# A wait that paces VectorE by GpSimd, and a sparser order of convolution taps, layer norm and top-k, in a two-layer hybrid decoder step on one core

## The reference

```python
def mixer_layer(x, c, q_pos, top_k, ...):
    shift, scale, gate = jnp.split(jax.nn.silu(c) @ w_ada + b_ada, 3, axis=-1)
    h = rms_norm(x, norm_g) * (1 + scale[:, None]) + shift[:, None]
    zq, zk, zv, zqi, zki, zwi, zga, zglu, zgc, zmerge = split_in(h @ w_in)
    ...
    attn = ...            # indexer scores, top-k keys per query, softmax over them
    y_att = (attn * jax.nn.silu(zga)) @ w_attn_out
    za, zb = jnp.split(zglu, 2, axis=-1)
    u = za * jax.nn.sigmoid(zb)
    d = lax.conv_general_dilated(conv_in, conv_w, ...) + conv_b     # causal, depthwise, 31 taps, 1024 channels
    d = layer_norm(d, conv_ln_g, conv_ln_b)
    y_conv = (jax.nn.silu(d) * jax.nn.silu(zgc)) @ w_conv_out
    g_att, g_conv = jnp.split(jax.nn.sigmoid(zmerge), 2, axis=-1)
    return x + gate[:, None] * ((g_att * y_att + g_conv * y_conv) @ w_out), ...
```

## Time and profile before

| | us |
|---|---|
| median of 3 runs | 3767.42 |
| lowest, highest | 3760.27, 3771.24 |
| the profiled execution | 3748.51 |
| its span | 3746.7 |
| PE busy | 3517.2 (94%) |
| DVE busy | 1797.4 (48%) |
| POOL busy | 1217.4 (32%) |
| ACT busy | 1065.2 (28%) |

### The profile page before, as it was taken

How to read it: one execution, slowest core, us unless ns; L and a number is a source line. 1 busy time by engine, 2 the same in 40 slices (tenths; PEclk the granted TensorE clock), 3 DMA queues, 4 the chain that set the end, 5 groups by cost and what they waited for, 6 DMA issues and landing times. The chain is left out here.

```text
span 3746.7 us, 66701 instructions
## 1 busy us (share of the span) xinstructions
PE 3517.2 (94%) x27774; PEld 3257.7 (87%) x27774; DVE 1797.4 (48%) x2508; ACT 1065.2 (28%) x1494; POOL 1217.4 (32%) x476
## 2 busy tenths in 40 slices
PE   5699999989899899999998999998988999999999
PEld 2499988878889889898887999897888898889999
DVE  0422578946888412322114135789189791233311
ACT  1322222222353233221213222222233523332221
POOL 0133333543323222333232333235333232224433
PEclk9799999999999999999998999999999999999999
DMA  9733334555544675558994555442332246744442
GB/s 302 232 110 103 95 103 110 158 146 175 153 125 123 198 238 193 173 194 262 307 294 132 159 158 166 135 120 77 94 98 85 72 131 221 241 136 134 131 127 93
DMA packets 556513, 590.47 MB, mean 158 GB/s; under 512 B 73432, under 2 KB 523245, under 8 KB 546475
## 3 DMA queue, kind: packets, MB, share of 16 engines
q1 hardware_dynamic: 556212, 586.21, 51.5%
HBM read 546.37 MB, written 116.39 MB: 177 GB/s over the span
## 5 line engine op out<-in xcount | busy, mean ns | idle before, releaser
L781 POOL TENSOR_TENSOR w_lo_t<-raw,w_hi_t 128x1024 fp32r<-128x1024 f32 x472 | 1217.2, 2579 | 2512.9 <-ACT w_hi_t L790 2512.9
L1067 PE MATMUL acc<-act_hi,w_hi_t 128*128 128x272 f32 x6528 | 1414.3, 298 | 112.9 <-POOL w_lo_t L781 38.0
L1067 PE MATMUL acc<-act_hi,w_lo_t 128*128 128x272 f32 x6528 | 1361.4, 290 | 0.0
L1067 PE MATMUL acc<-act_lo,w_hi_t 128*128 128x272 f32 x6528 | 1359.9, 290 | 0.0
L1067 PEld LDWEIGHTS acc<-act_hi,w_hi_t 128*128 128x128 f32 x6528 | 1040.9, 191 | 201.2 <-issue 131.6
L1067 PEld LDWEIGHTS acc<-act_lo,w_hi_t 128*128 128x128 f32 x6528 | 1039.4, 191 | 0.0
L1067 PEld LDWEIGHTS acc<-act_hi,w_lo_t 128*128 128x128 f32 x6528 | 1032.6, 191 | 0.0
L790 ACT ACTIVATE w_hi_t<-raw 128x1024 fp32r<-128x1024 f32 x472 | 499.9, 1059 | 1665.6 <-PE acc L1067 1662.7
L1067 PE MATMUL acc<-m_hi,w_hi_t 128*128 128x272 f32 x1024 | 215.8, 292 | 0.0
L1590 DVE SCALAR_TENSOR_TENSOR conv<-conv,cw 128x512 f32<-128x512 f32 x240 | 212.2, 884 | 0.0
L1067 PE MATMUL acc<-m_hi,w_lo_t 128*128 128x272 f32 x1024 | 211.5, 288 | 0.0
(11 more groups left out here) (240 smaller groups left out, 2711.5 us busy)
## 6 DMA issues: line engine op xcount, KB each, us to landing
raw<-in_w_in_dram SPq DMA_DIRECT2D x272, 512.0 KB, 3.7
ada_ring<-in_w_ada_dram SPq DMA_DIRECT2D x94, 512.0 KB, 6.3
raw<-in_w_in_dram SPq DMA_DIRECT2D x136, 256.0 KB, 3.3
k_near<-in_cache_k_dram SPq DMA_DIRECT2D x256, 128.0 KB, 2.7
v_near<-in_cache_v_dram SPq DMA_DIRECT2D x256, 128.0 KB, 2.7
k_ring<-k_near SPq DMA_DIRECT2D x64, 512.0 KB, 5.3
v_page<-v_near SPq DMA_DIRECT2D x64, 512.0 KB, 6.1
raw<-in_w_out_dram SPq DMA_DIRECT2D x64, 512.0 KB, 4.6
```

The costliest lines, as they stand in the source:

```text
L781: pool.tensor_tensor(w_lo_t[:, m % 2], raw[:, m % 4], w_hi_t[:, m % 2].bitcast(F32), ALU.subtract).then_inc(S.w_lo, 1)
L1067: last = pe.matmul(acc[:, 2 * m + h, 0:HALF], w[:, c % 2, k, P * m:P * m + P], r[:, kt, h * HALF:(h + 1) * HALF], start=first and k == 0 a ...
```

## The change

VectorE gets a wait in front of the taps of every odd half slot: w_lo must have counted the chunk after the one to which the half slot belongs. The taps from half slot 64 on go at 27 per 7 half slots instead of 16 per 5, so the last one is in half slot 107 instead of 116. The norm's H_SUM goes from 117 to 109, and its first part (the sum) from half slot 117 to 108. top_p begins at 121 instead of 130, with 2.5 rounds per half slot instead of 3 (last in 140 instead of 145). Prompt attention begins at 142 instead of 146. top_s begins in 141 instead of 146 and ends in 196 instead of 197.

```diff
-H_SUM = 117
-H_TOPP = 130
-H_LP = 146
+H_SUM = 109
+H_TOPP = 121
+H_LP = 142
...
-    return min(CT_ * TAPS, 80 + 16 * (h - 63) // 5)
+    return min(CT_ * TAPS, 82 + (27 * (h - 64) + 6) // 7)
...
-    return max(0, min(3 * 16, 3 * (h - H_TOPP + 1)))
+    return max(0, min(3 * 16, 5 * (h - H_TOPP + 1) // 2))
...
-    if h < H_LP:
-        return 0
     if h < H_LP + 28:
-        return h - H_LP + 1
-    return min(64, 28 + (3 * (h - H_LP - 27) + 1) // 2)
+        return max(0, h - H_TOPP - 19)
+    return min(64, 30 + (5 * (h - H_LP - 27) + 3) // 4)
...
-                if s == 0:
+                if s == -1:
...
-                for t in range(taps_by(h - 1), taps_by(h)):
+                taps = range(taps_by(h - 1), taps_by(h))
+                if taps and h % 2 == 1:
+
+                    dve.wait_ge(S.w_lo, w_chunk(l, N_GLU, 0) + h // 2 + 2)
+                for t in taps:
                     tap(l, t)
```

## The result

| | kernel before | changed kernel |
|---|---|---|
| median of the timed runs | 3769.33 us (3760.27 to 3773.77) | 3674.59 us (3673.25 to 3676.36) |
| profiled execution | 3748.51 us, span 3746.7 | 3676.36 us, span 3674.6 |
| ratio of the medians, 95% | | 0.9752 (0.9737 to 0.9767) |

The predicted time was 3675.0. The two profiled executions are only 72 us apart, and the medians 95.

The account below looks back on a forecast made before the run. It took TensorE, busy 94% of the span, as the bound, with only its stalls worth removing. Two layers of 25.8 + 21.9 - 1.5 us gave 92, taken from the median 3767.4: 3675 us, range 3657 to 3727.

Parts of the forecast that it names:

- Term A: Half slots 68 to 101: the wait removes TensorE's three stalls for GpSimd's low halves, 25.8 us a layer, bounds 17 and 26.
- The hold of up to 8 us: From half slot 64, until VectorE catches up, a hold may last three half slots (8 us); no stall taken.
- Its reason: Half slots 68 to 101: back-to-back taps hold GpSimd's subtraction until VectorE drains; spread taps plus subtraction, 7.7 us, fit 8.49.
- Rival 1: A run of taps delays a subtraction by one tap at most; the 15 us have another cause and stay: 3724 us, 8%.
- Waits in half slots 8 to 63: VectorE's early waits for the low half cost nothing, with 1 us to spare before make_u in 40 to 63.
- Rival 3: Half slots 8 to 63: the wait puts VectorE and GpSimd in lock step, make_u comes late: slower, 3809 us, 6%.
- Nothing won at the sum: Sum at half slot 108 instead of 117: TensorE waits 5 us instead of 5.8; the 4.3 us gate stall stays.
- Rival 2: VectorE reaches the sum 8 us a layer later than reckoned and everything behind moves along: 3691 us, 12%.
- Top-k: Earlier top_p rounds cut TensorE's 9.91 us wait at the second L1210 group to 0 to 3: 8.9 us a layer.
- Bias: At the k transposes: bias ready in time, first transpose to logits 17.8 us instead of 30.8: 13.0 us a layer.
- The sum: Both layers: 2 x (25.8 + 21.9 - 1.5) = 92 us, subtracted from the median 3767.4, giving 3675 us.

Follow-up runs that it names:

- e1: Kernel before with only VectorE's wait for the next low half added, taps, sum and top-k left in place: 3702.04 us, ratio 0.9847.
- e7: Kernel before, with VectorE waiting for its own last tap at every sixth tap, no wait for GpSimd: 3702.47 us, ratio 0.9819.
- e2: Changed kernel without the wait for the low half, keeping the earlier taps, sum and top-k: 3735.26 us, ratio 0.9940 to the kernel before.
- e3: Changed kernel with the wait made only from half slot 64 on: 3670.67 us, ratio 0.9735 to the kernel before.
- e4_again: Changed kernel with SyncE's bias store at half slot 198 and bias loads at 200 and 204: 3653.78 us, ratio 0.9725 to the kernel before.
- e10: e4_again with sum, mean and norm two half slots later (H_SUM 111 for 109), top-k unmoved: 3652.66 us, ratio 0.9725 to the kernel before.
- e11: e4_again with a VectorE wait for its own last tap every sixth tap replacing the low-half wait: 3649.23 us, ratio 0.9720 to the kernel before.
- e8: Kernel before, with GpSimd making each low-half subtraction of half slots 66 to 102 twice: 3719.88 us, ratio 0.9866.
- e5: Kernel before with the first two taps of each channel made two-input operations like the other 29: 3762.68 us, ratio 1.0014.

## Why the prediction was right, point by point

- **Term A, 25.8 us a layer: right.** 76.82 us became 51.6, stage 64–102 fell by 25.2 us (25.1 in the first layer), and e1 gives 25.9 alone. The hold of up to 8 us at the beginning of these half slots came as well: one of 8.04 is left, and it cost 0.7 us of a step where none was taken.
- **Its reason: half right.** That a hold ends at VectorE's gap, and that pacing removes it, was shown by e1, e7 and e2. What was left open, why some runs hold and others don't, goes by the taps since the last gap or handover. The rule cited (the Trainium skill, "SBUF — State Buffer", Who interferes with whom: the first to issue holds the shared pair for its instruction) agrees with the 99 subtractions let in after at most one tap, and fails for the 27 that let 16 to 22 taps by. Rival 1, built on it, is refuted by e1.
- **Waits in half slots 8 to 63 at nothing: nothing shown against it** (e3, where up to some 4 us isn't excluded). Rival 3, the slower one, had no part.
- **Nothing won at the sum: nearly.** A wait of 4.2 us for 5.8, with the gate at 4.3 as foretold. Rival 2 did not happen.
- **Top-k, 8.9 us a layer: right in kind, low.** The wait of 9.9 is gone altogether; half slots 102 to 196 fell by 12.6 us, where the steps gave 8.9 less 1.5 for held subtractions. Of the 2.7 us beyond the 9.9, 1.6 are ln_sum's; the rest was not traced.
- **Bias, 13.0 us a layer: the step that failed.** The bias is in time, but the step from there to "18 us from first k transpose to logits" was wrong. Its reason, "with four raw buffers it is free before TensorE has used them up", looks at the weights alone, and no row shows TensorE stopped by those. It did not count the 8.4 us of bias and v loads that stand behind the store, nor that the next k_ring loads stand behind those: TensorE stood 7.6 us for its keys. The 13.0 us measured 2.4 (78.53 to 76.17). e4_again shows the missing part, 9.8 us, and with it 12.1.
- **The sum.** 46.2 us a layer predicted, 40.2 to 40.9 found: 81 for 92. The time came out within 0.4 us because the 92 were taken from a median 19 us above the profile, on the argument that the offset would stay. It did not: the change's profile lies 1.8 us above its own median. Two errors, of 11 and 14 us, nearly cancelled. That the time came out so closely is luck; the direction and the larger term are not.

## What to carry to other kernels

When GpSimd and VectorE both read SBUF, a long row of back-to-back two-input operations on VectorE can shut GpSimd out until the row ends: here from eight such operations of 0.66 us on. Look for GpSimd operations several times their normal length, read the idle time before them, and put a gap of some 0.04 us (a wait for VectorE's own last operation) into the row every six or so. When a step is moved earlier in a DMA queue past an engine that is late, count how long the queue stands there and everything that it issues in the same step, since the loads behind it are late by the sum. A wait that is removed ahead of a late engine can come back at that engine's next product: e10 made one stage 12 us shorter, the next 14 us longer, and won nothing.

## What was not expected of the hardware

- A gap prevents a hold, and doesn't only end it: with a gap every sixth tap, all 50 subtractions that came into taps after 5.2 to 6.5 us of GpSimd's idle time (e7, e11) took 2.39 to 2.93 us.
- Doing work twice on GpSimd made the kernel 1.3% faster (e8).
- At 4.41 us of idle time a subtraction was let in after two taps in the kernel before, after six in the changed one (5.66 us) and after ten in e5 (8.28 us): the border lies there and is not to be planned on.
